# Turning the residual x in the branch product and adding it by VectorE after the output product

## The chip, the cores and the metric

The kernel runs on one core of a Trainium2 chip (trn2). The metric is the device time of one execution in microseconds (us); lower is better. A core has TensorE (PE: matmuls, and separately PEld: its weight loads), VectorE (DVE), ScalarE (ACT), GpSimd (POOL) and SyncE (SP), each with its own instruction stream, which meet at semaphores, and 16 DMA engines that all queues share. Queue q1 carries what SP issues, q10 what ScalarE issues, q0 what GpSimd issues.

## The reference

One layer of a decoder over 520 tokens (512 of a prompt, 8 samples), model width 1024, all float32. What matters here is the end of the mixer and the start of the feed-forward part:

```python
yb = jax.nn.silu(layernorm(yb + conv_b_bias, ln_b_g, ln_b_b)) @ w_out_b
...
g = jax.nn.sigmoid(gate_logits + b_gate).reshape(bsz, t, N_BRANCH, D_MODEL)
merged = g[:, :, 0] * ya + g[:, :, 1] * yb + g[:, :, 2] * yx
h = x + merged @ w_o

hn = rmsnorm(h, norm_ffn)
h = h + (jax.nn.silu(hn @ w_ff_gate) * (hn @ w_ff_up)) @ w_ff_down
```

`x` is what the change is about: it lies in memory as rows of tokens, while the kernel keeps every activation turned, channels on the 128 partitions and tokens along them, so `x` must be turned before it can be added.

## The kernel before

**Tiles.** Every product has its weights cut into chunks of 256 output channels, that is two tiles of 128, by 1024 inputs (8 steps of k). A float32 product is made from three products of rounded parts: weights `w_h` by activations high and low, then the weights' rest `w_l` by the activations' high part. Per k and tile that is two matmuls of 260 tokens for each pairing. `chunk` runs a whole chunk: `tile_hi` for both tiles (line 1467, 64 matmuls), then `tile_lo` for both (line 1483, 32 matmuls). The accumulators are four PSUM tiles `acc0` to `acc3`, used in turn by numbered uses (`number_uses`); `free(use)` makes TensorE wait until the use four before has been read (`acc_read`), `done(use)` makes a reader wait for TensorE (`acc_done`).

**Weights.** They have two slots. SP loads a chunk into `w_raw` (line 383, 1 MB, queue q1) as soon as the rest of the chunk two before has landed in the same slot. ScalarE makes `w_h` (line 490, twice) and minus `w_raw` in `w_l` (line 492) when TensorE has finished with the slot (`split`); then GpSimd issues an accumulating DMA that leaves the rest in `w_l` (line 474, 1 MB, queue q0). `tile_lo` waits for its landing.

**Stages in question.** The branch product (`C_OB`, four chunks of `w_out_b`, activations `zb`): VectorE multiplies each tile by its gate (line 1339) and adds it to `merged` (line 1342), ScalarE rounds `merged` to `br[0]` (line 788), VectorE makes the low part `br[1]` (line 1334). Then the output product (`C_WO`, four chunks of `w_o`, activations `br`). Its accumulators also get `x`: after `tile_lo`, TensorE multiplies slices of `x_st` (the rows of `x_prompt`) and `xs_st` (`x_sample`) by an identity into the same accumulator (lines 1711 and 1713), which turns and adds them at once; 10 matmul records of the first form and 2 of the second for a tile, since each float32 matmul is done in two. `x_st` and `xs_st` are loaded by five DMAs that ScalarE issues (lines 793 and 794) once the last branch tile is done, since `x_st` lies over `zb`. TensorE waits for all five (`x_again`) before the first identity product. The readers are then ScalarE (its square, line 804, and the scaled high part `hg[0]`, line 807) and VectorE (a copy to `h_sb`, line 1352, the sum of squares `hsum`, line 1357, the low part `hg[1]`, line 1358, which also frees the accumulator). The feed-forward gate product (`C_F`) takes `hg` as activations, one k at a time as they get ready; `mean` then sums `hsum` over the partitions.

The order on each engine is written out by hand; nothing is moved by a scheduler.

Of the kernel before, what the change touches and what calls it, by code (L numbers as in the profile page):

```python
# [19 lines left out]
P = 128  # L20
# [31 lines left out]
def number_uses():  # L52
# [43 lines left out]
    use("ob", 8)  # L96
# [10 lines left out]
def decoder_step(nc, x_prompt, x_sample, mem_prompt, cache_mem_k, cache_mem_v, state_conv_a,  # L107
# [68 lines left out]
    x_st = at("x_st", [P, 4, D], f32, o_p2h)  # L176
    nrm_2 = at("nrm_2", [P, KT, P], f32, o_p2h)
    xs_st = at("xs_st", [TS, D], f32, o_p2l)
# [77 lines left out]
    with ctx:  # L256
# [75 lines left out]
        x_again = sem("x_again")  # L332
        h_hi = sem("h_hi")
# [20 lines left out]
        def turn(c):  # L354

            if isinstance(c, int):
                return (c - C_B) // 2 + 1
            i, per_pass, offset = c
            return i * (per_pass // 2) + ((offset - C_B) // 2 + 1)

# [6 lines left out]
        def f(ap):  # L367

            return ap.bitcast(f32)
# [112 lines left out]
        def _(act):  # L482
# [301 lines left out]
            for n in range(KT):  # L784
                if n % 2 == 0:
                    split(C_OB + n // 2 + 1, (n // 2 + 1) % 2, T["ob"] + n - 1)
                act.wait_ge(m_sum, n + 1)
                nc.scalar.activation(br[0][:, n, :], merged[:, n, :], ACT.Copy).then_inc(m_hi, 1)


            done(T["ob"] + 7)
            for t in range(4):
                act.dma_start(x_st[:, t, :], x_prompt[0, t * P:(t + 1) * P, :]).then_inc(x_again, 16)
            act.dma_start(xs_st[:, :], xs_dram).then_inc(x_again, 16)


            for n in range(KT):
                if n % 2 == 0:
                    split(C_WO + n // 2 + 1, (n // 2 + 1) % 2, T["wo"] + n - 1)
                use = T["wo"] + n  # L800
                done(use)
                if n >= 2:
                    act.wait_ge(h_sum, n - 1)
                nc.scalar.activation(two(sg[:, n % 2, 0:TOK]), halves(use), ACT.Square).then_inc(h_sq, 1)
                if n == 0:
                    act.wait_ge(m_lo, KT)
                nc.scalar.activation(two(hg[0][:, n, :]), halves(use), ACT.Copy,
                                     scale=prm[:, n, R_FFN:R_FFN + 1]).then_inc(h_hi, 1)
# [69 lines left out]
        def _(dve):  # L878
# [456 lines left out]

            dve.wait_ge(gb_sig, KT)
            for n in range(KT):
                done(T["ob"] + n)
                V.tensor_tensor(two(sgB[:, n, :]), halves(T["ob"] + n), two(sgB[:, n, :]), ALU.mult) \
                    .then_inc(acc_read, 1 if n else 3)  # L1340
                dve.wait_ge(acc_read, T["ob"] + n + 1)
                V.tensor_tensor(merged[:, n, :], merged[:, n, :], sgB[:, n, :], ALU.add).then_inc(m_sum, 1)
                if n:
                    m_lo_part(n - 1)
            m_lo_part(KT - 1)


            for n in range(KT):
                use = T["wo"] + n
                done(use)  # L1350
                dve.wait_ge(h_hi, n + 1)
                V.tensor_copy(two(h_sb[:, n, :]), halves(use))
                if n == 0:
                    V.tensor_copy(hsum[:, :], sg[:, 0, 0:TOK]).then_inc(h_sum, 1)
                else:
                    dve.wait_ge(h_sum, n)
                    V.tensor_tensor(hsum[:, :], hsum[:, :], sg[:, n % 2, 0:TOK], ALU.add).then_inc(h_sum, 1)
                V.scalar_tensor_tensor(two(hg[1][:, n, :]), halves(use), param(n, R_FFN), two(f(hg[0][:, n, :])),
                                       ALU.mult, ALU.subtract).then_inc(acc_read, 1)
# [70 lines left out]
        def _(pe):  # L1430
# [255 lines left out]
            for j in range(4):  # L1686
                chunk(C_OB + j, j % 2, T["ob"] + 2 * j, T["ob"] + 2 * j, zb, None if j else (z_lo, 0))


            for c in range(4):  # L1690
                def halves_of(s, c=c):
                    return 2 * (C_WO + c) + s + 1

                for j in range(2):
                    use = T["wo"] + 2 * c + j
                    free(use)
                    tile_hi(c % 2, j, use, br, ready=None if c + j else (m_lo, 0),
                            first_half=None if j else halves_of)
                for j in range(2):
                    tile_lo(c % 2, j, T["wo"] + 2 * c + j, br, stop=False, loaded=None if j else C_WO + c)  # L1700
                if c == 0:
                    pe.wait_ge(x_again, 16 * 5)
                for j in range(2):
                    use = T["wo"] + 2 * c + j
                    cols = slice((2 * c + j) * P, (2 * c + j + 1) * P)
                    for t in range(4):

                        for b in range(2):
                            a, z = max(t * P, b * HALF), min((t + 1) * P, (b + 1) * HALF)
                            if a < z:  # L1710
                                M.matmul(acc[use % 4][:, b, a - b * HALF:z - b * HALF], x_st[:, t, cols],  # L1711
                                         ident[:, a - t * P:z - t * P], start=False, stop=b == 0 and z == HALF)
                    M.matmul(acc[use % 4][:, 1, HALF - TS:HALF], xs_st[:, cols], ident[0:TS, 0:TS],
                             start=False, stop=True).then_inc(acc_done, 1)


            chunk(C_F, 0, T["fg"], T["fg"], hg, (acc_read, T["wo"]))
# [69 lines left out]
```

## Time and profile before

| | us |
|---|---|
| Median of 3 runs (1162.33 to 1164.49) | 1162.92 |
| The profiled execution | 1165.77 |
| Its span in the trace | 1164.0 |
| TensorE matmuls busy in it | 1108.7 (95%) |
| VectorE busy | 526.6 (45%) |
| ScalarE busy | 494.0 (42%) |
| GpSimd busy | 118.3 (10%) |

All times in the trace are us from the start of the span. The stages in question lie from 655 (the branch product at full pace) to 780 (the second chunk of the feed-forward product). A matmul's duration contains its latency, so the pace of TensorE is read from the distance between starts. TensorE's clock has two levels there, 2.4 GHz (a granted clock of 1.00) and 1.2 GHz (0.50).

### The profile page before, as it was taken

What the parts mean: (1) busy time and instruction counts of PE and PEld (TensorE: products, weight loads), DVE (VectorE), ACT (ScalarE), POOL (GpSimd) and SP (SyncE); (2) the same over time, 40 slices, a digit from 0 to 9 for tenths busy, and PEclk for the clock granted to TensorE, in tenths of its full rate; (3) what the DMA queues carried; (4) which work ended last, traced back from release to release, by engine and by line L of the source; (5) the groups of instructions that cost most, each with busy time, mean ns of one, the idle gap of its engine ahead of it and who ended that gap; (6) DMA issues with size and microseconds to landing.
All of it is one profiled execution on the core that took longest, in us unless ns stands there. A gap on an engine that the chain in (4) does not pass through costs nothing.

```text
span 1164.0 us, 20989 instructions
## 1 busy us (share of the span) xinstructions
PE 1108.7 (95%) x9036; PEld 1098.7 (94%) x9036; DVE 526.6 (45%) x916; ACT 494.0 (42%) x546; POOL 118.3 (10%) x114
## 2 busy tenths in 40 slices
PE   4998999999799999999999999999999999999994
PEld 3998999899799999999999999999999999999994
DVE  5642766874977745585433532233232223200113
ACT  4444434333432543343346733444343534343242
POOL 4740000000000000000000000000000000000000
PEclk9998999999899999999999998999999999999998
DMA  7578875679788778668876687547777777777762
GB/s 257 180 216 234 204 195 135 181 217 268 169 231 228 177 177 202 182 152 192 201 203 147 169 206 218 132 123 181 191 193 185 185 180 183 180 199 199 173 150 96
DMA packets 131838, 217.99 MB, mean 187 GB/s; under 512 B 4724, under 2 KB 118452, under 8 KB 120751
## 3 DMA queue, kind: packets, MB, share of 16 engines
q0 software_dynamic: 12384, 90.18, 38.8%
q1 hardware_dynamic: 98006, 102.89, 27.4%
q10 hardware_dynamic: 21385, 24.01, 6.2%
q8 instruction: 48, 0.79, 0.3%
q14 instruction: 15, 0.12, 0.0%
HBM read 122.40 MB, written 5.47 MB: 110 GB/s over the span
## 4 chain that ended last, share of the span: by engine, by line
PE 80%; DVE 9%; DMA 5%; ACT 3%; ACTq 1%; issue 1%; SPq 0%; DVEq 0%
PE acc L1467 47%; PE acc L1483 25%; PE acc L1527 2%; PE acc L1440 2%; DMA v_st<-in_cache_mem_v_dram 2%; DVE k_st L1096 1%; DVE ubyb L1024 1%; PE acc L1534 1%; DMA w_l<-w_raw 1%; PE acc L1602 1%; ACT w_h L490 1%; DMA xs_st<-in_x_sample_dram 1%; PE acc L1711 1%; DMA prow<-in_ln_b_b_dram 1%; ACTq L647 1%
## 5 line engine op out<-in xcount | busy, mean ns | idle before, releaser
L1467 PE MATMUL acc<-big_h,w_h 128*128 128x260 f32 x2016 | 411.0, 285 | 3.8 <-DVE sg L1203 2.5
L1467 PE MATMUL acc<-big_l,w_h 128*128 128x260 f32 x2016 | 407.1, 283 | 0.0
L1467 PEld LDWEIGHTS acc<-big_h,w_h 128*128 128x128 f32 x2016 | 312.5, 190 | 5.6 <-DVE sg L1203 2.4
L1467 PEld LDWEIGHTS acc<-big_l,w_h 128*128 128x128 f32 x2016 | 312.9, 190 | 0.0
L490 ACT ACTIVATE w_h<-w_raw 128x1024 fp32r<-128x1024 f32 x188 | 188.2, 1050 | 229.5 <-PE acc L1483 116.4
L1483 PE MATMUL acc<-big_h,w_l 128*128 128x260 f32 x2016 | 257.6, 285 | 6.2 <-DMA w_l<-w_raw 6.2
L1483 PEld LDWEIGHTS acc<-big_h,w_l 128*128 128x128 f32 x2016 | 251.0, 191 | 6.8 <-DMA w_l<-w_raw 6.6
L1024 DVE SCALAR_TENSOR_TENSOR ubyb<-ubyb,prm 128x512 f32<-128x512 f32 (+1 forms) x240 | 180.3, 751 | 15.2 <-DVE ubyb L1024 9.4
L474 POOL DMA_DIRECT2D w_l<-w_raw x86 | 73.1, 850 | 984.7 <-ACT w_l L492 973.4
L492 ACT ACTIVATE w_l<-w_raw 128x2048 fp32r<-128x2048 f32 x86 | 163.6, 1902 | 0.0
L1467 PE MATMUL acc<-hg_h,w_h 128*128 128x260 f32 x704 | 142.2, 283 | 1.4 <-DVE sg L1367 1.3
L1467 PE MATMUL acc<-hg_l,w_h 128*128 128x260 f32 x704 | 141.4, 282 | 0.0
L1467 PEld LDWEIGHTS acc<-hg_h,w_h 128*128 128x128 f32 x704 | 108.2, 188 | 1.8 <-DVE sg L1367 1.5
L1467 PEld LDWEIGHTS acc<-hg_l,w_h 128*128 128x128 f32 x704 | 108.4, 188 | 0.0
L1483 PE MATMUL acc<-hg_h,w_l 128*128 128x260 f32 x704 | 88.0, 282 | 0.0
L1483 PEld LDWEIGHTS acc<-hg_h,w_l 128*128 128x128 f32 x704 | 86.0, 188 | 0.0
L1408 DVE TENSOR_TENSOR h_sb<-acc,h_sb 128x520 f32<-128x520 f32 x8 | 5.6, 700 | 117.5 <-PE acc L1483 117.5
L1367 DVE TENSOR_TENSOR sg<-acc,rms 128x520 f32<-128x520 f32 x22 | 15.3, 699 | 83.9 <-PE acc L1483 83.8
L1378 DVE TENSOR_TENSOR sg<-acc,sg 128x520 f32<-128x520 f32 x22 | 15.4, 700 | 78.8 <-PE acc L1483 78.8
L470 POOL TENSOR_TENSOR w_l<-w_raw,w_h 128x1024 fp32r<-128x1024 f32 x16 | 43.9, 2765 | 28.7 <-ACT w_h L490 28.7
L818 ACT ACTIVATE sgf<-sg 128x520 f32<-128x520 f32 x22 | 14.0, 639 | 67.5 <-DVE sg L1367 67.5
L822 ACT ACTIVATE big_h<-sg 128x520 f32 (+1 forms) x22 | 14.1, 640 | 65.5 <-DVE sg L1378 65.5
(191 smaller groups left out, 794.4 us busy)
## 6 DMA issues: line engine op xcount, KB each, us to landing
w_l<-w_raw POOLq DMA_DIRECT2D x86, 1024.0 KB, 7.6
w_raw<-in_w_in_dram SPq DMA_DIRECT2D x36, 1024.0 KB, 5.3
w_raw<-in_w_ff_gate_dram SPq DMA_DIRECT2D x11, 1024.0 KB, 5.3
w_raw<-in_w_ff_up_dram SPq DMA_DIRECT2D x11, 1024.0 KB, 5.2
k_st<-in_cache_mem_k_dram ACTq DMA_DIRECT2D x8, 1024.0 KB, 5.0
v_st<-in_cache_mem_v_dram ACTq DMA_DIRECT2D x8, 1024.0 KB, 13.1
w_raw<-in_w_ff_down_dram SPq DMA_DIRECT2D x8, 1024.0 KB, 5.1
w_raw<-in_w_k_dram SPq DMA_DIRECT2D x4, 1024.0 KB, 10.9
```

The source lines that it names most:

```text
L470: nc.gpsimd.tensor_tensor(w_l[:, c % 2, ks, :], w_raw[:, c % 2, ks, :], f(w_h[:, c % 2, ks, :]), ALU.subtract).then_inc(kv_w_lo, 1)
L474: pool.dma_start(w_l[:, c % 2, :, :].rearrange("p k n -> p (k n)"), w_raw[:, c % 2, :, :].rearrange("p k n -> p (k n)"), accum_op=ALU.add) ...
L490: nc.scalar.activation(w_h[:, slot, ks, :], w_raw[:, slot, ks, :], ACT.Copy).then_inc(w_hi, 1)
L492: nc.scalar.activation(w_l[:, slot, :, :], w_raw[:, slot, :, :], ACT.Copy, scale=-1.0) \
L822: nc.scalar.activation(mid_f[0][:, bass.ds(i * (2 * TOK) + j * TOK, TOK)], sg[:, j, 0:TOK], ACT.Copy).then_inc(f_hi, 1)
L1024: ins = V.scalar_tensor_tensor(y, u, w, y, ALU.mult, ALU.add)
L1367: V.tensor_tensor(two(sg[:, j, 0:TOK]), halves(gate + j), two(rms[:, :]), ALU.mult) \
L1378: V.tensor_tensor(two(sg[:, j, 0:TOK]), halves(up + j), two(sg[:, j, 0:TOK]), ALU.mult) \
L1440: return M.transpose(out, src, ident[0:rows, 0:rows])
L1467: last = M.matmul(out[:, b, 0:HALF], w_h[:, slot, k, cols], xs[:, k_at + k, b * HALF:(b + 1) * HALF], start=start and k == 0 and xs is x[0 ...
L1483: last = M.matmul(out[:, b, 0:HALF], w_l[:, slot, k, cols], x[0][:, k_at + k, b * HALF:(b + 1) * HALF], start=False, stop=stop and k == ks ...
L1527: M.matmul(acc[use % 4][:, m, 0:CW], mn[n][:, k, rows], w_h[:, c % 2, k, :], start=k == 0 and n == 0, stop=False)
```

## The change

`x` is loaded while the branch product runs: ScalarE issues the five DMAs behind the weight split for the branch product's second chunk, and only then rounds the first `merged`. To allow that, `x_st` lies over the first third of the activation buffer (`xn`, whose last reader is the gate product before the branch product), `xs_st` over the convolution's buffer. After each of the four branch chunks TensorE turns two tiles of `x` by plain transposes (`flip`) into the two accumulators that are free; VectorE copies them to a new tile `xT`. In the output product the identity matmuls are gone and each chunk is an ordinary `chunk`. VectorE reads an output tile once, adding `xT` into `h_sb`, and that frees the accumulator; ScalarE and VectorE then make `hg` and the squares from `h_sb` in SBUF instead of from PSUM. The feed-forward product waits for the low parts by a semaphore of its own, `g_lo`.

```diff
@@ -93,7 +93,9 @@
     use("ctail")
     use("a", 16)
     use("gb", 10)
-    use("ob", 8)
+    for j in range(4):
+        use(f"ob{j}", 2)
+        use(f"xt{j}", 2)
     use("wo", 8)
     use("fg", 2)
     use("r")
@@ -173,9 +175,10 @@
     mid = [b[:, 0:FT * TOK].rearrange("p (k t) -> p k t", t=TOK) for b in (big_h, big_l)]
     mid_f = [b[:, 0:FT * TOK] for b in (big_h, big_l)]
     o_p2h, o_p2l = o_bh + 8 * ACTV, o_bl + 8 * ACTV
-    x_st = at("x_st", [P, 4, D], f32, o_p2h)
+    x_st = at("x_st", [P, 4, D], f32, o_bh)
+    xT = at("xT", [P, KT, TOK], f32, o_bl)
     nrm_2 = at("nrm_2", [P, KT, P], f32, o_p2h)
-    xs_st = at("xs_st", [TS, D], f32, o_p2l)
+    xs_st = at("xs_st", [TS, D], f32, o_ub)
     hsum = at("hsum", [P, TOK], f32, o_p2l + 4 * D)
     tail = 4 * FT * TOK
     rms = at("rms", [P, TOK], f32, o_bh + tail)
@@ -330,6 +333,7 @@
         m_hi = sem("m_hi")
         m_lo = sem("m_lo")
         x_again = sem("x_again")
+        g_lo = sem("g_lo")
         h_hi = sem("h_hi")
         h_sq = sem("h_sq")
         h_sum = sem("h_sum")
@@ -357,6 +361,9 @@
                 return (c - C_B) // 2 + 1
             i, per_pass, offset = c
             return i * (per_pass // 2) + ((offset - C_B) // 2 + 1)
+
+        def ob(n):
+            return T[f"ob{n // 2}"] + n % 2
         z_tmp = [ubyb[:, KT, 0:TOK], sg[:, 0, 0:TOK]]
@@ -783,29 +790,27 @@
             for n in range(KT):
                 if n % 2 == 0:
-                    split(C_OB + n // 2 + 1, (n // 2 + 1) % 2, T["ob"] + n - 1)
+                    split(C_OB + n // 2 + 1, (n // 2 + 1) % 2, ob(n) - 3 if n else T["gb"] + 9)
+                if n == 0:
+                    for t in range(4):
+                        act.dma_start(x_st[:, t, :], x_prompt[0, t * P:(t + 1) * P, :]).then_inc(x_again, 16)
+                    act.wait_ge(z_lo, KT)
+                    act.dma_start(xs_st[:, :], xs_dram).then_inc(x_again, 16)
                 act.wait_ge(m_sum, n + 1)
                 nc.scalar.activation(br[0][:, n, :], merged[:, n, :], ACT.Copy).then_inc(m_hi, 1)
-            done(T["ob"] + 7)
-            for t in range(4):
-                act.dma_start(x_st[:, t, :], x_prompt[0, t * P:(t + 1) * P, :]).then_inc(x_again, 16)
-            act.dma_start(xs_st[:, :], xs_dram).then_inc(x_again, 16)
-
-
             for n in range(KT):
                 if n % 2 == 0:
-                    split(C_WO + n // 2 + 1, (n // 2 + 1) % 2, T["wo"] + n - 1)
-                use = T["wo"] + n
-                done(use)
+                    split(C_WO + n // 2 + 1, (n // 2 + 1) % 2, T["wo"] + n - 1 if n else ob(7))
+                act.wait_ge(acc_read, T["wo"] + n + 1)
+                if n == 0:
+                    act.wait_ge(m_lo, KT)
+                nc.scalar.activation(hg[0][:, n, :], h_sb[:, n, :], ACT.Copy,
+                                     scale=param(n, R_FFN)).then_inc(h_hi, 1)
                 if n >= 2:
                     act.wait_ge(h_sum, n - 1)
-                nc.scalar.activation(two(sg[:, n % 2, 0:TOK]), halves(use), ACT.Square).then_inc(h_sq, 1)
-                if n == 0:
-                    act.wait_ge(m_lo, KT)
-                nc.scalar.activation(two(hg[0][:, n, :]), halves(use), ACT.Copy,
-                                     scale=prm[:, n, R_FFN:R_FFN + 1]).then_inc(h_hi, 1)
+                nc.scalar.activation(sg[:, n % 2, 0:TOK], h_sb[:, n, :], ACT.Square).then_inc(h_sq, 1)
             def middle(i, u_gate, u_up, root=False):
@@ -1333,30 +1338,46 @@
                 dve.wait_ge(m_hi, n + 1)
                 V.tensor_tensor(br[1][:, n, :], merged[:, n, :], f(br[0][:, n, :]), ALU.subtract).then_inc(m_lo, 1)
+            def x_copy(n):
+                use = T[f"xt{n // 2}"] + n % 2
+                done(use)
+                V.tensor_copy(xT[:, n, 0:TP], acc[use % 4][:, 0, :])
+                V.tensor_copy(xT[:, n, TP:TOK], acc[use % 4][:, 1, 0:TS]).then_inc(acc_read, 1)
+
             dve.wait_ge(gb_sig, KT)
             for n in range(KT):
-                done(T["ob"] + n)
-                V.tensor_tensor(two(sgB[:, n, :]), halves(T["ob"] + n), two(sgB[:, n, :]), ALU.mult) \
+                done(ob(n))
+                V.tensor_tensor(two(sgB[:, n, :]), halves(ob(n)), two(sgB[:, n, :]), ALU.mult) \
                     .then_inc(acc_read, 1 if n else 3)
-                dve.wait_ge(acc_read, T["ob"] + n + 1)
+                dve.wait_ge(acc_read, ob(n) + 1)
                 V.tensor_tensor(merged[:, n, :], merged[:, n, :], sgB[:, n, :], ALU.add).then_inc(m_sum, 1)
                 if n:
                     m_lo_part(n - 1)
+                if n % 2:
+                    x_copy(n - 1)
+                    x_copy(n)
             m_lo_part(KT - 1)
-            for n in range(KT):
-                use = T["wo"] + n
-                done(use)
+            def h_parts(n):
                 dve.wait_ge(h_hi, n + 1)
-                V.tensor_copy(two(h_sb[:, n, :]), halves(use))
+                V.scalar_tensor_tensor(hg[1][:, n, :], h_sb[:, n, :], param(n, R_FFN), f(hg[0][:, n, :]),
+                                       ALU.mult, ALU.subtract).then_inc(g_lo, 1)
+                dve.wait_ge(h_sq, n + 1)
                 if n == 0:
                     V.tensor_copy(hsum[:, :], sg[:, 0, 0:TOK]).then_inc(h_sum, 1)
                 else:
                     dve.wait_ge(h_sum, n)
                     V.tensor_tensor(hsum[:, :], hsum[:, :], sg[:, n % 2, 0:TOK], ALU.add).then_inc(h_sum, 1)
-                V.scalar_tensor_tensor(two(hg[1][:, n, :]), halves(use), param(n, R_FFN), two(f(hg[0][:, n, :])),
-                                       ALU.mult, ALU.subtract).then_inc(acc_read, 1)
+
+            dve.wait_ge(acc_read, T["wo"])
+            for n in range(KT):
+                use = T["wo"] + n
+                done(use)
+                V.tensor_tensor(two(h_sb[:, n, :]), halves(use), two(xT[:, n, :]), ALU.add).then_inc(acc_read, 1)
+                if n:
+                    h_parts(n - 1)
+            h_parts(KT - 1)
             def middle(i, u_gate, u_up, gate, up, release):
@@ -1684,37 +1705,22 @@
             for j in range(4):
-                chunk(C_OB + j, j % 2, T["ob"] + 2 * j, T["ob"] + 2 * j, zb, None if j else (z_lo, 0))
+                chunk(C_OB + j, j % 2, T[f"ob{j}"], T[f"ob{j}"], zb, None if j else (z_lo, 0))
+                if j == 0:
+                    pe.wait_ge(x_again, 16 * 5)
+                for n in (2 * j, 2 * j + 1):
+                    use = T[f"xt{j}"] + n % 2
+                    free(use)
+                    for t in range(4):
+                        flip(acc[use % 4][:, 0, t * P:(t + 1) * P], x_st[:, t, n * P:(n + 1) * P])
+                    flip(acc[use % 4][:, 1, 0:TS], xs_st[:, n * P:(n + 1) * P]).then_inc(acc_done, 1)
             for c in range(4):
-                def halves_of(s, c=c):
-                    return 2 * (C_WO + c) + s + 1
-
-                for j in range(2):
-                    use = T["wo"] + 2 * c + j
-                    free(use)
-                    tile_hi(c % 2, j, use, br, ready=None if c + j else (m_lo, 0),
-                            first_half=None if j else halves_of)
-                for j in range(2):
-                    tile_lo(c % 2, j, T["wo"] + 2 * c + j, br, stop=False, loaded=None if j else C_WO + c)
-                if c == 0:
-                    pe.wait_ge(x_again, 16 * 5)
-                for j in range(2):
-                    use = T["wo"] + 2 * c + j
-                    cols = slice((2 * c + j) * P, (2 * c + j + 1) * P)
-                    for t in range(4):
-
-                        for b in range(2):
-                            a, z = max(t * P, b * HALF), min((t + 1) * P, (b + 1) * HALF)
-                            if a < z:
-                                M.matmul(acc[use % 4][:, b, a - b * HALF:z - b * HALF], x_st[:, t, cols],
-                                         ident[:, a - t * P:z - t * P], start=False, stop=b == 0 and z == HALF)
-                    M.matmul(acc[use % 4][:, 1, HALF - TS:HALF], xs_st[:, cols], ident[0:TS, 0:TS],
-                             start=False, stop=True).then_inc(acc_done, 1)
-
-
-            chunk(C_F, 0, T["fg"], T["fg"], hg, (acc_read, T["wo"]))
+                chunk(C_WO + c, c % 2, T["wo"] + 2 * c, T["wo"] + 2 * c, br, None if c else (m_lo, 0))
+
+
+            chunk(C_F, 0, T["fg"], T["fg"], hg, (g_lo, 0))
             pe.wait_ge(h_sum, KT)
             mean(T["r"], hsum)
             chunk(C_F + 1, 1, T["fu"], T["fu"], hg)
```

How the instructions stand, with the tiles' buffer numbers and the semaphores that each waits for. TensorE, around the end of the first branch chunk, before:

```order
L1483 MATMUL acc3<-big_h_52,w_l_51 128x260 [waits w_rest0]
L1483 MATMUL acc3<-big_h_52,w_l_51 128x260 x15
L1483 MATMUL acc0<-big_h_52,w_l_51 128x260 x16
L1467 MATMUL acc1<-big_h_52,w_h_50 128x260 [waits w_hi,acc_read]
L1467 MATMUL acc1<-big_h_52,w_h_50 128x260
L1467 MATMUL acc1<-big_l_53,w_h_50 128x260 x2
```

and in the changed kernel (its `flip` is line 1461, `tile_hi` 1488, `tile_lo` 1504; `x_st_54` and `xs_st_57` are the rows of x):

```order
L1504 MATMUL acc3<-big_h_52,w_l_51 128x260 [waits w_rest0]
L1504 MATMUL acc3<-big_h_52,w_l_51 128x260 x15
L1504 MATMUL acc0<-big_h_52,w_l_51 128x260 x16
L1461 MATMUL acc1<-ident_100,x_st_54 128x128 [waits acc_read,x_again]
L1461 MATMUL acc1<-ident_100,x_st_54 128x128 x3
L1461 MATMUL acc1<-ident_100,xs_st_57 128x8
L1461 MATMUL acc2<-ident_100,x_st_54 128x128 [waits acc_read]
L1461 MATMUL acc2<-ident_100,x_st_54 128x128 x3
L1461 MATMUL acc2<-ident_100,xs_st_57 128x8
L1488 MATMUL acc3<-big_h_52,w_h_50 128x260 [waits w_hi,acc_read]
```

The wait for x (`x_again`) stands now behind the first of the four branch chunks, with ten transposes behind it; before, it stood behind the first output chunk.

ScalarE, from the weight split for the second branch chunk on, before (the five loads of x come 12 rows further down, behind the last rounding of `merged`):

```order
L490 ACTIVATE w_h_50<-w_raw_49 128x1024 [waits acc_done,w_loaded1]
L490 ACTIVATE w_h_50<-w_raw_49 128x1024
L492 ACTIVATE w_l_51<-w_raw_49 128x2048
L788 ACTIVATE big_h_52<-merged_61 128x520 [waits m_sum] x2
L490 ACTIVATE w_h_50<-w_raw_49 128x1024 [waits acc_done,w_loaded0]
```

and in the changed kernel:

```order
L497 ACTIVATE w_h_50<-w_raw_49 128x1024 [waits acc_done,w_loaded1]
L497 ACTIVATE w_h_50<-w_raw_49 128x1024
L499 ACTIVATE w_l_51<-w_raw_49 128x2048
L796 DMA x_st_54<-in_x_prompt_dram 128x1024 x4
L798 DMA xs_st_57<-in_x_sample_dram 8x1024 [waits z_lo]
L800 ACTIVATE big_h_52<-merged_62 128x520 [waits m_sum] x2
L497 ACTIVATE w_h_50<-w_raw_49 128x1024 [waits acc_done,w_loaded0]
```

The five loads moved ahead of the first two roundings of `merged`, three chunks earlier.

VectorE, at the last two output tiles, before:

```order
L1357 TENSOR_TENSOR hsum_57<-hsum_57,sg_93 128x520 [waits h_sum]
L1358 SCALAR_TENSOR_TENSOR hg_l_88<-acc1,prm_100,hg_h_87 128x520
L1352 COPY h_sb_64<-acc2 128x520 [waits h_hi,acc_done]
L1357 TENSOR_TENSOR hsum_57<-hsum_57,sg_93 128x520 [waits h_sum]
L1358 SCALAR_TENSOR_TENSOR hg_l_88<-acc2,prm_100,hg_h_87 128x520
L1388 RECIPROCAL rms_58<-rms_58 128x520 [waits r_root,h_sum]
```

and in the changed kernel:

```order
L1377 TENSOR_TENSOR h_sb_65<-acc2,xT_55 128x520 [waits acc_done]
L1364 SCALAR_TENSOR_TENSOR hg_l_89<-h_sb_65,prm_101,hg_h_88 128x520 [waits h_hi]
L1371 TENSOR_TENSOR hsum_58<-hsum_58,sg_94 128x520 [waits h_sum,h_sq]
L1364 SCALAR_TENSOR_TENSOR hg_l_89<-h_sb_65,prm_101,hg_h_88 128x520 [waits h_hi]
L1371 TENSOR_TENSOR hsum_58<-hsum_58,sg_94 128x520 [waits h_sum,h_sq]
L1409 RECIPROCAL rms_59<-rms_59 128x520 [waits r_root,h_sum]
```

The read of the accumulator stands now first and no longer waits for ScalarE (`h_hi`); the low part of the tile before comes behind it.

## Rows read from the trace of the kernel before

**Rows 1.** Chain that ended last, branch and output products: start us, us, what.

```profile
663.35 7.66 PE acc L1467 x64
...
674.84 7.66 PE acc L1467 x64
...
716.24 9.32 PE acc L1467 x64
...
732.45 7.88 PE acc L1467 x64
...
747.22 7.88 PE acc L1467 x64
```

**Rows 2.** Timeline of PE, 697 to 766: start, us, what, [idle before].

```profile
697.66 0.40 PE L1467 MATMUL acc<-big_h,w_h 128*128 128x260 f32 x2
...
711.37 1.39 PE L1711 MATMUL acc<-ident,x_st 128*128 128x128 f32 x10 [2.05 <-DMA xs_st<-in_x_sample_dram]
...
761.92 0.51 PE L1467 MATMUL acc<-hg_h,w_h 128*128 128x260 f32 x2
```

**Rows 3.** Windows: us, busy (x) of PE PEld DVE ACT POOL, PEclk, DMA, GB/s.

```profile
293.00:296.00 3.00, 0.00 (x0) 0.00 (x0) 2.87 (x6) 1.00 (x2) 0.00 (x0) 1.00 0.50 104
296.10:299.60 3.50, 3.50 (x16) 3.50 (x17) 3.39 (x7) 2.70 (x2) 0.51 (x1) 0.51 0.65 188
99.40:102.40 3.00, 0.02 (x1) 0.02 (x1) 0.00 (x0) 0.00 (x0) 0.00 (x0) 0.87 0.68 172
102.40:108.40 6.00, 6.00 (x27) 6.00 (x28) 0.70 (x1) 3.80 (x3) 0.50 (x1) 0.50 0.56 179
...
712.60:719.40 6.80, 6.80 (x31) 6.44 (x30) 3.54 (x6) 4.32 (x7) 0.00 (x0) 0.50 0.58 153
```

**Rows 4.** Chain, 1081 to 1083: ten transposes between two chunks.

```profile
1081.07 1.09 PE acc L1440 x10
```

**Rows 5.** Timeline of ScalarE: last split, first roundings, the loads of x.

```profile
656.52 1.90 ACT L492 ACTIVATE w_l<-w_raw 128x2048 fp32r<-128x2048 f32 x1
663.04 0.64 ACT L788 ACTIVATE big_h<-merged 128x520 fp32r<-128x520 f32 x1 [4.62 <-DVE merged L1342]
...
699.38 2.13 ACTq L793 DMA_DIRECT2D x_st<-in_x_prompt_dram  x4
```

**Rows 6.** Timeline of GpSimd: the accumulating DMAs of branch chunks two, three.

```profile
658.71 0.85 POOL L474 DMA_DIRECT2D w_l<-w_raw  x1 [8.77 <-ACT w_l L492]
669.48 0.84 POOL L474 DMA_DIRECT2D w_l<-w_raw  x1 [9.92 <-ACT w_l L492]
```

**Rows 7.** DMA queues, 660 to 665: packets, MB, share of the 16 engines.

```profile
q0 software_dynamic: 126, 1.03, 100.5%
q1 hardware_dynamic: 117, 0.10, 6.7%
```

**Rows 8.** DMA queues, 705 to 709, x beside a weight load.

```profile
q10 hardware_dynamic: 332, 1.23, 78.5%
q1 hardware_dynamic: 335, 0.34, 24.4%
```

**Rows 9.** Timeline of VectorE, last output tile: copy from PSUM, low part.

```profile
763.59 0.69 DVE L1352 COPY h_sb<-acc 128x520 f32<-128x520 f32 x1
...
764.80 0.76 DVE L1358 SCALAR_TENSOR_TENSOR hg_l<-acc,prm,hg_h 128x520 fp32r<-128x520 f32 x1
```

**Rows 10.** Timeline of ScalarE, an issue while an accumulating DMA is running.

```profile
343.57 1.93 ACTq L647 DMA_DIRECT2D v_st<-in_cache_mem_v_dram  x2
```

**Rows 11.** DMA queues, 345 to 347, all rows.

```profile
q0 software_dynamic: 39, 0.32, 114.0%
```

**Rows 12.** DMA queues, 353 to 357.

```profile
q0 software_dynamic: 90, 0.74, 88.5%
q1 hardware_dynamic: 80, 0.08, 7.5%
q10 hardware_dynamic: 98, 0.10, 7.5%
```

## The prediction

> **What bounds the kernel now.** I read part 1 of the page first: TensorE's matmuls are busy 1108.7 of 1164.0 us and no other engine reaches half, so a time can only come out of what TensorE does not need to do, or of its waits. Next comes the chain of waits around the two products that the change touches [rows 1]. One chunk of the branch product takes 11.49 us (from 663.35 to 674.84: 64 matmuls in 7.66, then 32 in 3.83). Four chunks of the output product would be 45.96 us at that pace, but from the first output matmul at 697.66 to the first feed-forward matmul at 761.92 it is 64.26 us [rows 2]. The difference, **18.3 us**, is what x costs now. The timeline of TensorE shows its first piece, a wait of 2.05 us for x to land [rows 2]. The windows show the second: after that wait the granted clock is 0.50, its 1.2 GHz level, from 712.6 to 719.4 [rows 3]. Behind the output product TensorE runs chunk after chunk to the end, so what is won or lost before 761.92 arrives at the end in full.
>
> **What is removed.** The wait, 2.05 us. The first pair of identity products, from 711.37 to 716.24: 4.87. The half clock in the next chunk: its 64 matmuls took 9.32 and not 7.66, so 1.66 [rows 1, 2]. The three later pairs: from 732.45 to 747.22 a chunk with its pair takes 14.77, that is 3.28 more than 11.49, three times 9.84 [rows 1]. Together 18.4, which agrees with the 18.3 from both ends. I take 18.3.
>
> **What is added on TensorE.** Ten transposes after each branch chunk. Ten transposes of the same shapes stand between two chunks near the end and take 1.09 us on the chain [rows 4]; with the change of kind at the next chunk 1.1, four times **4.4 us**. They are on the path, nothing covers them. They need two free accumulators, which come free when VectorE has multiplied the chunk's first tile by its gate; that tile is done 1.9 us (half of 3.83) before the chunk ends and the read of such a tile takes 0.69 [rows 1, 9], so no wait.
>
> **Where the load of x now stands.** This decides. ScalarE finishes the split for the second branch chunk at 656.52 + 1.90 = 658.42 [rows 5] and issues x then; before, it did so at 699.38. TensorE is through with the first branch chunk at 663.35 [rows 1] and then stands at x. So the load has 4.9 us of cover. Before, from the first issue at 699.38 to the first identity product at 711.37 it took 12.0 us [rows 2, 5]. Even that unchanged would end at 670.4, 7 us late.
>
> It won't be unchanged, as an accumulating DMA of 1 MB for the second branch chunk is issued at 658.71, beside x [rows 6]. Count the 16 engines' time from 660. That DMA takes 100.5% of five us, 5.0 us; the tail of a weight load 0.3 (6.7% of five) [rows 7]. x is four DMAs of 512 KB and one of 32 KB, 2.13 MB; at 1.23 MB for 78.5% of four us it costs 5.4 us [rows 8]. The next weight load is released by the accumulating DMA's landing and takes 24.4% while x runs [rows 8], some 0.6 us. Sum: 660 + 0.3 + 5.0 + 5.4 + 0.6 = **671.3**, if the engines never stand idle. That is the lower bound. The upper one: the 12.0 us of before hold 5.4 for x and, at the same rate per MB, 2.7 for a 1 MB weight load; 3.9 us were start-up and gaps. If the start-up comes after the accumulating DMA with nothing beside it, x lands at up to 675. For that speaks an issue of 2 MB from ScalarE at 343.57, in the middle of such a DMA: from 345 to 347 queue q0 alone moved packets, q10 none [rows 10, 11]. I take 672.5, nearer the lower end, since here the accumulating DMA is issued 0.3 us behind x and not ahead of it. **The new wait is 672.5 - 663.35 = 9.15 us.**
>
> On how queues share the engines, the Trainium skill (DMA: Bandwidth & Descriptors, Queues, rings and completion order) says that each DMA engine takes turns between the queues that have work, a packet at a time; by it x would start to move at once and the wait end at 671.3, 1.2 us less in the sum. The row from 353 to 357 agrees, with 90, 80 and 98 packets on the three queues [rows 12]; the one from 345 to 347 does not.
>
> **The clock after the wait.** TensorE stood for 3 us before 296 and then ran 3.5 us at 0.51; it stood for 3 us before 102.4 too and then ran 6.0 us at 0.50; after the wait of 2.05 us it was 6.8 us [rows 2, 3]. Work at half the clock costs half its time: 1.75 to 3.4 us. The wait here is longer than all of these; I take 6.0 us of half clock, **3.0 us**.
>
> **What moves at no cost.** ScalarE issues after 658.42, 2.13 us for four [rows 5] and about a quarter of that for the fifth; its next instruction ran at 663.04, after a wait for VectorE [rows 5], and the issues are through by 661.2. Behind them stands the split for the third branch chunk, whose time doesn't move. VectorE has eight pairs of copies more, the long one of each about as long as a read of a tile at 0.69 [rows 9]; two of them join the six instructions of that length in each chunk of 11.49 us, some 6 us of work in all. During the new wait VectorE stands at its first copy, with the second tile pair behind it, which TensorE has not made yet either.
>
> **The seam to the feed-forward product.** When the last output tile is done, VectorE adds it (0.69), makes the low part of the tile before (0.76), adds a square (as long as the first) and makes the last low part (0.76): 2.9 us [rows 9]; ScalarE's high part lies beside it. TensorE wants that last k only after seven steps of four matmuls at 7.66/64 = 0.12, that is 3.35 us. No wait, with 0.45 us to spare.
>
> **Sum.** -18.3 + 9.15 + 4.4 + 3.0 = -1.75 us. The profiled execution took 1165.77 us (span 1164.0), so it would be 1164.0; the median of the runs is 1162.92, which gives 1162.92 - 1.75 = **1161.2 us**. With the bounds (x landed at 671.3 and 1.75 for the clock; 675 and 3.4) its own range is 1158.7 to 1164.1. So the change takes 18 us of work and stall away from the output product and puts most of it back as a stall two chunks earlier.
>
> **Rivals.**
> - *x goes first.* ScalarE's first issue is 0.3 us ahead of GpSimd's [rows 5, 6]. If x passes whole before the accumulating DMA, it lands at 660.3 + 5.4 = 665.7, the wait is 2.35 us, and the time 1162.92 - 18.3 + 2.35 + 4.4 + 3.0 = 1154.4. The second chunk's weight rest would land later, but is needed only 1.1 + 7.66 us after the wait. Against it: x's four issues take 2.1 us, and most of x stands behind the other queue's packets by then. 0.10.
> - *x is caught by the next accumulating DMA (slower than before).* The one for the third branch chunk is issued at 669.48 [rows 6], and while one runs beside q10, that queue moves 98 packets in 4 us [rows 12]. x has packets of 3.7 KB (1.23 MB in 332) [rows 8]. If more than some 125 of them (0.46 MB) are left when it begins, x trickles for its whole 5 us and lands at about 677.5: a wait of 14.15 us, +3.25 us, 1166.2. It decides at a landing of 676.6; from there on the kernel is slower by 0.2%. For it speaks that x has no time to spare: the DMA issued at 658.71 was at full share from 660 [rows 6, 7], so the next would begin at about 670.8. Against it, by the sum above x then has half a us left, 50 packets. 0.20.
> - *The seam waits.* If a VectorE or ScalarE step there is a us longer than the rows say, TensorE waits half a us to one, 1162. 0.06.
> - *The forecast.* 0.64.
>
> **How the numbers follow.** A measurement of this kernel can tell about 0.2%, 2.3 us, from no change; that is below 1160.6 or above 1165.2. The forecast's own case lies across the first of these: 0.29 faster, 0.33 same, 0.02 slower. x first adds 0.10 to faster. The trickle adds 0.16 to slower and 0.04 to same, the seam 0.06 to same. So 0.39 faster, 0.43 same, 0.18 slower. The range goes from somewhat below the forecast's own lower end to just above the trickle's time, 1157.0 to 1166.5; x first is left out.
>
> **What would show it.** In the profile of the changed kernel: an idle time of 8 to 11 us ahead of the first transpose, released by the DMA of `xs_st`; a granted clock of 0.50 behind it for 3 to 7 us; ten transposes in 1.1 us after the second to fourth branch chunks; output chunks 11.5 us apart with no matmul from `ident`; the first feed-forward matmul at about 760. If the first transpose starts before 668, the sharing of the queues is what I got wrong, in the kernel's favour; after 676, against it. If the idle time is as forecast and the total still differs by more than 2 us, the error is in the clock or in the seam.

## The result: faster by 0.8 to 1.2%, and TensorE hardly waits for x

| | before | changed |
|---|---|---|
| Median of 12 runs each, us | 1164.53 | 1157.28 |
| Profiled execution, us (span) | 1165.77 (1164.0) | 1155.19 (1153.5) |
| TensorE matmuls busy, us | 1108.7 | 1095.1 |
| From the `w_l` part of the first branch chunk to the first feed-forward matmul, us | 102.57 | 90.90 |
| From there to the end of the span, us | 402.08 | 401.63 |

The ratio is 0.9917, with a 95% interval of 0.9898 to 0.9936. The changed kernel was timed twice more beside other runs: 0.9879 (0.9847 to 0.9911) and 0.9897 (0.9872 to 0.9923). The forecast was 1161.2 us, 0.15% below the median known then (1162.92), with a range that began at 1157.0. The twelve runs of before lie in two groups, eight from 1162.3 to 1166.5 us and four from 1170.6 to 1173.0, while those of the changed kernel lie together from 1155.2 to 1159.3; so the medians are 7.25 us apart (0.6%) and the means 9.2 (0.8%). The stage alone gives -11.67 us and what follows it -0.45, together **-12.1 us** in the two profiles, where the forecast had -1.75. (The spans differ by 10.5, since the changed kernel's profile arrives at this stage 1.6 us later.)

(The fourth row is the yardstick for all runs below. The moment at which a run arrives at that `w_l` part moves between 659.35 and 663.97 us from profile to profile; the changed kernel's own lie at 660.97, 661.85 and 662.81, so whole spans of single profiles are not compared.)

The chain of waits of the changed kernel over the two products, to be held against [rows 1]; columns: start us, us, what:

```profile
655.27 0.38 ACTq L796
...
657.86 7.21 DMA xs_st<-in_x_sample_dram
665.08 0.04 issue
665.12 1.55 PE acc L1461 x10
666.67 7.88 PE acc L1488 x64
674.55 3.84 PE acc L1504 x32
678.40 1.33 PE acc L1461 x10
...
717.55 7.66 PE acc L1488 x64
725.21 3.84 PE acc L1504 x32
...
752.03 7.66 PE acc L1488 x64
```

The first branch chunk ends at 660.97 + 4.00 = 664.97 and the first transpose starts at 665.12: a wait of 0.15 us where 9.15 was forecast. There is no half clock behind it, as this window shows (us, busy (x) of PE PEld DVE ACT POOL, granted clock, DMA, GB/s):

```profile
664.00:668.00 4.00, 3.85 (x30) 3.27 (x29) 3.58 (x7) 1.28 (x2) 0.00 (x0) 1.00 1.07 252
```

The output chunks are 11.5 us apart and the feed-forward product follows without a stop. A pair of transposes takes 1.33 us and the next chunk 0.22 more (7.88 for 7.66), 1.55 in all, where the forecast had 1.1.

Why x had landed is in the timeline of ScalarE (ACT: its engine; ACTq: its instruction stream issuing a DMA):

```profile
655.13 0.64 ACT L763 ACTIVATE big_h<-ubyb 128x520 fp32r<-128x520 f32 x1 [0.64 <-DVE ubyb L1328]
655.27 0.38 ACTq L796 DMA_DIRECT2D x_st<-in_x_prompt_dram  x1
655.67 0.68 ACT L743 ACTIVATE sgB<-acc,prm 128x520 f32<-128x520 f32 x1
655.68 1.01 ACTq L796 DMA_DIRECT2D x_st<-in_x_prompt_dram  x1
656.25 1.05 ACT L497 ACTIVATE w_h<-w_raw 128x1024 fp32r<-128x1024 f32 x1
...
658.15 1.90 ACT L499 ACTIVATE w_l<-w_raw 128x2048 fp32r<-128x2048 f32 x1
```

and in that of GpSimd:

```profile
660.34 0.85 POOL L481 DMA_DIRECT2D w_l<-w_raw  x1 [8.77 <-ACT w_l L499]
```

The first load of x is issued at 655.27, when four activations that stand ahead of it in the program (L743, twice L497, L499) have not begun. The last of them ends at 660.05. By the order of instructions none of the four has to wait at a semaphore any more by then; the instruction stream evidently has handed them over to the engine and gone on to the DMAs. The accumulating DMA of GpSimd waits for the last activation's end and comes 5.1 us behind x. The DMA queues (packets, MB, share of the 16 engines) show what that means. First from 655 to 658, then from 658 to 662:

```profile
q0 software_dynamic: 64, 0.39, 74.5%
q10 hardware_dynamic: 28, 0.11, 19.2%
```

```profile
q10 hardware_dynamic: 441, 1.61, 99.9%
```

Until 656.8 the accumulating DMA of the first branch chunk has the engines; x moves its first packets at 657.2 and then has them for itself, 1.61 of its 2.13 MB in four us.

### The profile page after: what moved, and what is told of

It is laid out like the page before. It is cut to its first block, busy times and chain, and to the rows that moved or that the text cites. A ratio compares the mean times of both kernels' runs of the same rounds, so it can differ in the third digit from the quotient of the medians.

```text
span 1153.5 us, 20889 instructions
## 1 busy us (share of the span) xinstructions
PE 1095.1 (95%) x8980; PEld 1084.7 (94%) x8980; DVE 531.8 (46%) x932; ACT 494.2 (43%) x546; POOL 118.3 (10%) x114
## 4 chain that ended last, share of the span: by engine, by line
PE 77%; DMA 9%; DVE 7%; ACT 4%; issue 1%; ACTq 1%; POOL 0%; SPq 0%; DVEq 0%
PE acc L1488 47%; PE acc L1504 24%; DMA w_raw<-in_w_in_dram 3%; DMA w_l<-w_raw 3%; PE acc L1461 2%; ACT w_h L497 2%; DVE k_st L1101 1%; PE acc L1548 1%; PE acc L1623 1%; ACT w_l L499 1%; DMA prow<-in_ln_b_b_dram 1%; DVE ubyb L1029 1%; ACTq L654 1%; PE acc L1555 1%; DMA xs_st<-in_x_sample_dram 1%
## 5 line engine op out<-in xcount | busy, mean ns | idle before, releaser
L497 ACT ACTIVATE w_h<-w_raw 128x1024 fp32r<-128x1024 f32 x188 | 188.1, 1049 | 220.8 <-PE acc L1504 98.1
L499 ACT ACTIVATE w_l<-w_raw 128x2048 fp32r<-128x2048 f32 x86 | 163.4, 1901 | 0.0
## 6 DMA issues: line engine op xcount, KB each, us to landing
w_raw<-in_w_k_dram SPq DMA_DIRECT2D x4, 1024.0 KB, 11.2
```

The lines of the kernel that those rows point to most:

```text
L497: nc.scalar.activation(w_h[:, slot, ks, :], w_raw[:, slot, ks, :], ACT.Copy).then_inc(w_hi, 1)
L499: nc.scalar.activation(w_l[:, slot, :, :], w_raw[:, slot, :, :], ACT.Copy, scale=-1.0) \
```

## The experiments

The kernel before was timed again beside each group of experiments, and the ratios are to that: its median was 1170.11 us beside x_late, x_ahead and early_ident, 1168.76 beside no_x, after_again and wide_xs, 1168.46 beside sp_wide and after_third. Times in us are therefore compared only within a group. "The stretch" is the fourth row of the table above.

**x_late: x issued when the activations have ended.** One wait more in the changed kernel:

```diff
                 if n == 0:
+                    act.wait_ge(w_neg, C_OB + 2 - C_B)
                     for t in range(4):
                         act.dma_start(x_st[:, t, :], ...)
```

> The changed kernel with one wait more: ScalarE may issue the five loads of x only when its negation of the second branch chunk's weights has finished, which also releases GpSimd's accumulating DMA. Nothing else is changed. Theory A (in the changed kernel x was issued 2.9 us ahead of the end of that negation, so it went ahead of the accumulating DMA; which of the two is first decides): x now shares the DMA engines with the accumulating DMA, TensorE stands 7 to 12 us in front of the first transpose as the prediction had it, and with 2 to 3.4 us of half clock the time is 1157.3 + 9 to 15, that is 1166 to 1172. Theory B (only the later issue counts, the queues' order does not): the issue moves by 3 to 5 us, the wait is 3 to 5 us, and the time 1160 to 1165.

Measured: 1166.69 us median (10 runs), a ratio to before of 0.9982 (0.9961 to 1.0004). The issue is at 659.40 and the accumulating DMA at 659.67. Timeline of TensorE, then the queues from 661 to 663 and from 663 to 668, then windows around the restart:

```profile
673.27 1.12 PE L1462 MATMUL acc<-ident,x_st 128*128 128x128 f32 x4 [8.98 <-DMA xs_st<-in_x_sample_dram]
```

```profile
q10 hardware_dynamic: 136, 0.50, 65.6%
q0 software_dynamic: 16, 0.13, 31.5%
```

```profile
q0 software_dynamic: 109, 0.89, 88.8%
q10 hardware_dynamic: 67, 0.27, 14.0%
```

```profile
672.30:673.30 1.00, 0.03 (x1) 0.03 (x1) 0.00 (x0) 0.00 (x0) 0.00 (x0) 0.50 0.79 215
...
678.00:679.00 1.00, 1.00 (x7) 1.00 (x7) 0.00 (x0) 0.00 (x0) 0.00 (x0) 0.55 1.07 223
679.00:680.00 1.00, 1.00 (x10) 1.00 (x10) 0.00 (x0) 0.00 (x0) 0.00 (x0) 1.00 1.07 224
```

This is the kernel that the forecast described, and it behaves so: a wait of 8.98 us (9.15 forecast), half clock for 5.6 us from the restart (6.0), a time 0.18% below before (0.15%), which the interval does not tell from none. The stretch is 102.00 us, 11.1 more than in the changed kernel, though one wait is all that was added. Theory B (3 to 5 us of wait) falls: of the 8.8 us of longer wait, 4.8 are the later issue itself (it stands 0.9 us ahead of the `w_l` part and not 5.7), and 4.0 a longer way from the first issue to the first transpose, 13.9 us and not 9.9. The queues show the reason of Theory A for the 4.0, with one correction. x is issued first here too, by 0.27 us, and moves its first packets at 661.0; but from about 662.5 the accumulating DMA has most of the engines. So not who is first decides but the lead: 5.1 us was enough for most of x, 0.27 was not. (The weight load for the third branch chunk, behind x in the changed kernel, here has the engines from 659 to 661, 100.5%; how much of the 4.0 us it took is not separated.)

**x_ahead: the five loads written ahead of the split.**

```diff
                 if n == 0:
+                    for t in range(4): act.dma_start(x_st[:, t, :], ...)
+                    act.wait_ge(z_lo, KT)
+                    act.dma_start(xs_st[:, :], xs_dram)
                 if n % 2 == 0:
                     split(...)
-                if n == 0:
-                    ...
```

> The changed kernel with the five loads of x written ahead of the weight split of the second branch chunk instead of behind it. Theory A (ScalarE's instruction stream passes its engine: a DMA behind activations without a wait between is issued while they are still queued): the issue moves by less than 1 us and the time stays at 1157.3 within 0.2%. Theory B (the issue comes in the program's place and x was early for another reason): the issue moves ahead by about 3.8 us, the length of the split; TensorE does not wait for x in either, so a time below 1157 would have to come from the weight loads.

Measured: 1157.01 us median (4 runs), 0.9886 (0.9851 to 0.9922); the stretch is 91.38 us. Timeline of ScalarE:

```profile
657.47 0.64 ACT L763 ACTIVATE big_h<-ubyb 128x520 fp32r<-128x520 f32 x1 [0.64 <-DVE ubyb L1328]
657.48 1.52 ACTq L794 DMA_DIRECT2D x_st<-in_x_prompt_dram  x2
...
660.78 2.01 ACT L497 ACTIVATE w_h<-w_raw 128x1024 fp32r<-128x1024 f32 x2 [2.10 <-issue]
```

Three activations of 3.8 us have changed places with the loads, yet the issue stands 0.01 us behind the start of the last `big_h` rounding, against 0.14 in the changed kernel. It is a wait (of that rounding, for VectorE) that holds the stream, not the activations. What did move is the split: the engine now stood 2.10 us while its stream issued DMAs. Written behind the split, the loads are issued while the engine works it off.

**x_behind: x issued when the accumulating DMA has landed.** The wait is `act.wait_ge(w_rest[1], turn(C_OB + 1) * 16)` in the same place.

> The changed kernel, but ScalarE issues x only when the accumulating DMA of the second branch chunk has landed, so x runs without it. Theory A (start-up plus engine time): from the issue to the first transpose it takes 8 to 10 us, since the 12.0 us of the kernel before held a whole weight load; TensorE waits 11 to 14 us. If x takes 12 us even so, its start-up is the larger part of it. Behind a wait of this length the granted clock is at 0.50 when TensorE starts again; if a long wait costs no more than a short one, half clock lasts 3.4 to 7 us from there.

Measured: one execution of 1175.21 us, the stretch 108.16. Timeline of TensorE and a window behind it:

```profile
682.86 1.12 PE L1462 MATMUL acc<-ident,x_st 128*128 128x128 f32 x4 [15.08 <-DMA xs_st<-in_x_sample_dram]
```

```profile
688.00:689.00 1.00, 1.00 (x8) 1.00 (x8) 0.00 (x0) 0.00 (x0) 0.00 (x0) 0.72 0.44 122
```

From the first issue at 671.68 to the first transpose it took 11.2 us, more than the 8 to 10 expected and less than 12. The queues from 674 to 682 show all of x, and a weight load beside it again:

```profile
q10 hardware_dynamic: 591, 2.13, 68.5%
q1 hardware_dynamic: 813, 0.82, 29.8%
```

So 8 us are transfer (68.5% of it, 5.5 us, engine time of x), and 3.2 us lie before and behind it: the expectation's other case, that start-up is the larger part, did not come true. Half clock lasted from the restart into the window above, some 5.7 us, though the wait was 6 us longer than in x_late: between stops of 9 and 15 us, what the clock costs did not grow. (A single execution; only its trace is used.)

**early_ident: the early load alone.** The kernel before, with the loads at the new place and its identity products as they were:

```diff
-    x_st = at("x_st", [P, 4, D], f32, o_p2h)
+    x_st = at("x_st", [P, 4, D], f32, o_bh)
-    xs_st = at("xs_st", [TS, D], f32, o_p2l)
+    xs_st = at("xs_st", [TS, D], f32, o_bl)
```

> The kernel before with one part of the change: x is loaded at the branch product (the five loads behind the second weight split), but is still turned and added by identity products after the output chunks. It leaves the transposes and the copies out. If the gain of the change is load and product separately: gone are the wait of 2.05 us, the half clock behind it (1.66 in the next chunk and 1.6 in the first pair), together 5.3 us, so a ratio of about 0.9954 to the kernel before; the remaining 6.2 us or so of the change belong to transposes in place of identity products. If the clock falls anyway, 2 to 3 us only.

Measured: 1162.77 us median (7 runs), 0.9942 (0.9921 to 0.9963); the stretch is 97.73 us, 4.84 less than before. Chain of waits, then a row of TensorE's timeline:

```profile
657.17 14.82 DMA w_raw<-in_w_out_b_dram
...
676.13 7.38 DMA w_l<-w_raw
683.51 0.04 issue
683.55 4.09 PE acc L1484 x32
...
710.63 1.11 PE acc L1712 x10
```

```profile
683.55 1.22 PE L1484 MATMUL acc<-big_h,w_l 128*128 128x260 f32 x8 [0.20 <-DMA w_l<-w_raw]
```

The 5.3 us for wait and clock come as expected, less half a us. The rows show where most of that half us went, a new wait: the weight load for the third branch chunk stands behind x in the DMA engines and takes 14.82 us; what depends on it, the split and the accumulating DMA, lands at 683.51, when TensorE has stood 0.20 us (0.35 counted from start to start of its matmuls). In the changed kernel the transposes of two chunks give it 3 us more. The remaining 6.8 us of the change's 11.67 come with the rest of the change, mostly transposes in place of identity products.

**no_x: without x.** Loads, transposes and copies are out, and VectorE copies instead of adding; the residual is left out of the layer.

> The changed kernel without x: its loads, its transposes and their copies are left out, and VectorE copies the output tile instead of adding x. That leaves out the residual. If the changed kernel pays for x only with the four pairs of transposes (1.55 + 3 x 1.56 = 6.2 us, plus 0.15 of wait), this one is 6.4 us shorter, 1150.9. If the load of x costs something beside (later weight loads, waits elsewhere), it is shorter by more than that.

Measured: 1149.47 us median (6 runs), 0.9837 (0.9802 to 0.9871). Beside it, **after_again**, the changed kernel:

> The changed kernel unchanged, as the measure for the others of this call: a ratio of 0.990 to 0.994 to the kernel before, and no wait of TensorE over 0.5 us in front of the first transpose.

Measured: 1155.18 us median (6 runs), 0.9879, with a wait of 0.68 us in front of the first transpose, a little more than the half us expected. The medians are 5.7 us apart. The stretches are 84.29 and 91.28, so x costs 7.0 us there: 6.2 of transposes, the wait, and 0.1 left over. Its load costs nothing elsewhere that these rows show.

**wide_xs: transposes of one kind.**

```diff
-    xs_st = at("xs_st", [TS, D], f32, o_ub)
+    xs_st = at("xs_st", [P, D], f32, o_ub)
-                    flip(acc[use % 4][:, 1, 0:TS], xs_st[:, n * P:(n + 1) * P])
+                    flip(acc[use % 4][:, 1, 0:P], xs_st[:, n * P:(n + 1) * P])
```

> The changed kernel, but the tile of the sample rows has 128 partitions, of which 8 hold x_sample, and each of its eight transposes turns all 128; the 120 columns too many are not read. Theory A (the pair takes 1.55 us and not the 1.1 of the prediction because the transpose with 8 rows makes the weight load behind it wait, 0.17 us idle twice a pair on the weight side): the pair takes 1.1 us, -1.8 us in all, a ratio of 0.9985 to the changed kernel. Theory B (it is the two short instructions and their dispatch): no change within 0.3 us.

Measured: 1155.95 us median (6 runs), 0.9891 (0.9860 to 0.9922), beside after_again's 0.9879: the runs can't tell them apart. The chain of waits can:

```profile
681.31 1.09 PE acc L1461 x10
682.40 7.67 PE acc L1488 x64
690.07 3.84 PE acc L1504 x32
693.91 1.09 PE acc L1461 x10
```

A chunk with its pair takes 12.60 us where after_again has 13.02 and the changed kernel's first profile 13.05, and the stretch is 89.45 and not 91.28: 1.8 us less, as Theory A had it (0.15 of it is a shorter wait for x). As many transposes are there, so it is not their number. A transpose of 8 rows costs more than one of 128. In the changed kernel the weight side stands idle ahead of the weight load of each such transpose, and in wide_xs it does not (timeline of PEld); why it stands there is not shown:

```profile
678.76 0.13 PEld L1461 LDWEIGHTS acc<-ident,xs_st 8*128 8x128 f32 x1 [0.17 <-issue]
```

**sp_wide: a version meant to be better.** wide_xs, with the loads of x issued by SP:

```diff
+                if j == 2:
+                    sp.wait_ge(acc_done, T["gb"] + 10)
+                    for t in range(4):
+                        sp.dma_start(x_st[:, t, :], ...).then_inc(x_again, 16)
+                    sp.wait_ge(z_lo, KT)
+                    sp.dma_start(xs_st[0:TS, :], xs_dram).then_inc(x_again, 16)
                 load(C_OB + j, j % 2, wob, j * CW)
```

> A version meant to be better: the sample tile of 128 partitions (transposes of one kind), and SP issues the five loads of x, the first four as soon as the gate product before the branch product is done, ahead of the weight load of the third branch chunk, so that ScalarE issues nothing there. Expected against the changed kernel: 1.7 us from the transposes; the loads are issued about 3 us earlier, but the accumulating DMA of the first branch chunk is then still running, and if a newcomer's packets wait for it (as from 345 to 347 in the trace of before), x still starts when it ends and lands about 1 us earlier, which takes off the 0.2 to 0.9 us that TensorE waited there. Together 2 to 2.6 us, a ratio of 0.998 to the changed kernel. If the third chunk's weight load behind x comes late, part of it goes back.

Measured: 1154.57 us median (6 runs), 0.9882 (0.9861 to 0.9902). Beside it, **after_third**:

> The changed kernel again, as the measure for the run beside it: a ratio of 0.988 to 0.993 to the kernel before, a stretch from the last part of the first branch chunk to the first feed-forward matmul of 91 us.

Measured: 1155.93 us median (6 runs), 0.9897 (0.9872 to 0.9923), the stretch 91.22 us. That of sp_wide is 89.16, so 2.1 us less, of which 1.8 are the transposes. The issue begins at 654.27, in its timeline of SP, and TensorE still waits 0.22 us:

```profile
654.27 4.19 SPq L440 DMA_DIRECT2D x_st<-in_x_prompt_dram  x4
```

```profile
667.62 0.66 PE L1462 MATMUL acc<-ident,x_st 128*128 128x128 f32 x4 [0.22 <-DMA xs_st<-in_x_sample_dram]
```

Issued 9.1 us ahead of the `w_l` part and not 5.7 as in after_third, x came only 0.25 us earlier. The reason is the one expected, in the queues from 655 to 661: the accumulating DMA of the first branch chunk, issued at 653.16, was there, and x (here on q1) got little beside it:

```profile
q0 software_dynamic: 121, 0.92, 89.8%
q1 hardware_dynamic: 54, 0.22, 9.6%
```

The kernel is better by the stretch and by 1.4 us of median; the two intervals overlap, so it is not shown to be faster as a whole.

## Why the prediction was wrong, step by step

- **What is removed (18.3 us): right.** The output chunks follow at 11.5 us, and no wait, identity product or half clock is left there.
- **The issue of x: this step failed.** The prediction read the end of the split, 656.52 + 1.90 = 658.42 in [rows 5], as the moment of ScalarE's next instruction. In the changed kernel the issue came at 655.27, 4.8 us ahead of that split's end at 660.05. The trace of before had the evidence. In its timeline of ScalarE the activation ahead of the loads starts at 699.37, and the first load, in [rows 5], 0.01 us behind that start and not behind its end:

```profile
699.37 0.64 ACT L788 ACTIVATE big_h<-merged 128x520 fp32r<-128x520 f32 x1 [1.31 <-DVE merged L1342]
```

  Of this pair the prediction showed the load's row alone. There it makes 0.6 us; behind four activations it makes 4.8. The Trainium skill (Advanced Engine Details and Errata, Engine Queue Depths) gives ScalarE a queue of 8 instructions, which leaves room for the four seen here.
- **The wait (9.15 us): wrong for this kernel, right for the one described.** x_late, with the issue at the end of the split, waits 8.98. In the changed kernel it is 0.15, 0.68 and 0.47 in three profiles. It was a rival, x goes first, that came true, at a chance of 0.10 and with a wrong reason: it gave x 0.3 us of lead, and x has 5.1. With the lead that the rival had in mind x did not pass, as x_late shows. Its time, 1154.4, took a wait of 2.35 us and the half clock along, which did not come.
- **The clock (3.0 us): the same.** It did not fall; TensorE stood for 0.15 us only. Where it stopped for 9 us (x_late), the pair and the next chunk took 2.56 + 9.24 and not 1.55 + 7.84, so 2.4 us.
- **The transposes (4.4 us): mis-sized, 6.2 us.** The prediction took the ten of [rows 4] to be of the same shapes. They are not: their source is h_sb with 128 partitions each, and two of the ten of x have 8. wide_xs, with 128 in all, shows 1.09 us a pair.
- **The seam: right, and a little better.** No wait was forecast and there is none. What the sum left out is a wait of before, where the feed-forward chunk took 12.1 us to its end; it takes 11.7 now, the 0.45 us in the table above.
- **The trickle: did not come, and the sharing was half right.** In x_late x had 136 packets beside 16 at first and then 67 beside 109 in five us, so the queues did not take turns; and x was done at 672.8, before the next accumulating DMA, issued at 670.64, moved more than single packets.

With the right issue and sizes the same sum gives -18.3 + 0.15 + 6.2 - 0.45 = -12.4 us; the profiles show -12.1. Half of the difference is in how the wait is counted: from start to start of the matmuls it is 0.31 us.

## What to carry to other kernels

In these traces a DMA in ScalarE's instruction stream is issued when the last wait ahead of it is met, not when the work ahead of it is done, with up to four activations between; to date an issue, look for the last semaphore, not the last activation. That can be used both ways: place loads behind a block of work without waits and they run beside it, and add a wait only if they must not. When a load is moved, its time is set by its lead over the other large transfers, and being first by a fraction of a us did not help, so reckon both issues to a us before counting bandwidth. And a few short transposes in a run of long ones can cost more than long ones would.

## What the runs showed of the hardware that was not expected

- ScalarE's stream issued its first DMA with four activations (4.4 us of work) ahead of it in the program not yet begun. While it issues, it hands over no new activations: in x_ahead the engine stood 2.10 us.
- Of two transfers of 2 MB and 1 MB the accumulating one can hold the other back: with x issued 5.1 us ahead of it, x ran at 99.9% of the engines for four us; issued 0.27 us ahead (x_late), x had 14.0% for five us; issued 1.1 us behind one (sp_wide), 9.6% for six.
- After stops of 9 and 15 us TensorE ran at half clock for 5.6 and 5.7 us, no longer than the 6.8 after the stop of 2 us in [rows 3].
- The 2 MB load of x takes 9.85 us from first issue to use in the changed kernel (655.27 to 665.12), 11.2 in x_behind, 12.0 in the kernel before and 13.9 in x_late, of which its own engine time is 5.4 to 5.5; in x_behind, issued at 671.68 with the engines idle, its first packet moved at about 673.9.
